# Moving weight splits and convolution taps in the vector queue of a decoder step that TensorE bounds

## What is computed

```python
def conv_ffn(xn, buf, w_up, conv_w, conv_b, w_down):
    u = xn @ w_up                       # 1024 -> 2 x 3072
    g, v = u[..., :D_FF], u[..., D_FF:]
    gc, new_buf = causal_dwconv(g, buf, conv_w, conv_b)   # width 3, along the tokens
    return (jax.nn.gelu(gc) * v) @ w_down, new_buf.astype(buf.dtype)
```

## Time and profile before

| | us |
|---|---|
| median of 3 runs | 2318.5 |
| lowest and highest | 2316.89, 2319.08 |
| the profiled execution: own time | 2320.66 |
| its span, first to last instruction | 2318.6 |
| busy PE, weight loads of PE | 2293.2, 2235.5 |
| busy DVE, ACT, POOL | 1646.1, 1013.8, 1107.9 |

### The profile page before, as it was taken

One profiled execution on the slowest core, in us unless ns is written; L12 is line 12 of the kernel. 1 busy time (PEld: TensorE's weight loads), 2 busy tenths in 40 slices (PEclk: granted clock), 3 DMA queues, 4 the chain that ended last, 5 costly groups with the idle time before them and its releaser, 6 DMA issues.

```text
span 2318.6 us, 43248 instructions
## 1 busy us (share of the span) xinstructions
PE 2293.2 (99%) x16916; PEld 2235.5 (96%) x16916; DVE 1646.1 (71%) x2172; ACT 1013.8 (44%) x1732; POOL 1107.9 (48%) x922
## 2 busy tenths in 40 slices
PE   8999999999999999999999999999999999999999
PEld 8999999999999999999999867999999999999999
DVE  7666547777777779986466675467777777789962
ACT  6555645333333334433354585453333333444331
POOL 3222466555555555656220153565555555566540
PEclk9999999999999999999999999999999999999999
DMA  4111122222222334322373202222221222254132
GB/s 136 46 46 46 51 100 83 73 67 83 83 74 65 112 101 172 118 84 77 121 105 86 65 18 96 99 70 84 83 82 57 84 83 84 81 194 142 56 103 91
DMA packets 228790, 203.04 MB, mean 88 GB/s; under 512 B 28373, under 2 KB 209821, under 8 KB 228412
## 3 DMA queue, kind: packets, MB, share of 16 engines
q1 hardware_dynamic: 224180, 188.87, 26.3%
q10 hardware_dynamic: 4404, 12.28, 2.2%
q0 software_dynamic: 64, 0.05, 0.0%
HBM read 152.41 MB, written 50.66 MB: 88 GB/s over the span
## 4 chain that ended last, share of the span: by engine, by line
PE 90%; DVE 4%; issue 2%; ACT 2%; POOL 1%; DMA 1%; SPq 0%; DVEq 0%; ACTq 0%; POOLq 0%
PE ps L1473 14%; PE ps L1472 14%; PE ps L1474 14%; PE ps L1230 9%; PE ps L1232 9%; PE ps L1231 9%; PE ps L1492 4%; PE ps L1493 4%; PE ps L1494 4%; PE ps L1713 1%; PE ps L1741 1%; PE ps L1765 1%; PE ps L1636 0%; DVE y L2977 0%; PE ps L1813 0%
## 5 line engine op out<-in xcount | busy, mean ns | idle before, releaser
L1492 PE MATMUL ps<-ring,later_slots 128*128 128x272 f32 x960 | 277.9, 289 | 4.3 <-DVE later_slots L2999 2.5
L1493 PE MATMUL ps<-ring,later_slots 128*128 128x272 f32 x960 | 276.6, 288 | 0.0
L1494 PE MATMUL ps<-ring,later_slots 128*128 128x272 f32 x960 | 274.8, 286 | 0.0
L2977 DVE SCALAR_TENSOR_TENSOR y<-convin,fcol,y 128x1024 f32<-128x1024 f32 x192 | 227.5, 1225 | 16.4 <-ACT y L2193 14.7
L1472 PE MATMUL ps<-b,slot_a 128*128 128x272 f32 x768 | 221.5, 288 | 1.8 <-DVE slot_a L2931 1.8
L1473 PE MATMUL ps<-b,slot_a 128*128 128x272 f32 x768 | 221.2, 288 | 0.0
L1474 PE MATMUL ps<-b,slot_a 128*128 128x272 f32 x768 | 220.5, 287 | 0.0
L1492 PEld LDWEIGHTS ps<-ring,later_slots 128*128 128x128 f32 x960 | 180.8, 188 | 6.3 <-DVE later_slots L2999 4.0
L1494 PEld LDWEIGHTS ps<-ring,later_slots 128*128 128x128 f32 x960 | 181.5, 189 | 0.0
L1493 PEld LDWEIGHTS ps<-ring,later_slots 128*128 128x128 f32 x960 | 181.5, 189 | 0.0
L1230 PE MATMUL ps<-sa,whi 128*128 128x384 f32 (+1 forms) x540 | 177.3, 328 | 1.4 <-DVE x L3036 1.3
(11 more groups left out here) (503 smaller groups left out, 7885.6 us busy)
## 6 DMA issues: line engine op xcount, KB each, us to landing
rawu<-in_f_w_up SPq DMA_DIRECT2D x192, 256.0 KB, 4.3
h_spill<-x SPq DMA_DIRECT2D x48, 544.0 KB, 3.1
down_raw<-in_f_w_down SPq DMA_DIRECT2D x48, 384.0 KB, 4.6
part<-h_spill SPq DMA_DIRECT2D x30, 544.0 KB, 5.0
f_spill<-x ACTq DMA_DIRECT2D x16, 544.0 KB, 2.7
x<-f_spill SPq DMA_DIRECT2D x16, 544.0 KB, 6.8
raw<-in_a_w_in SPq DMA_DIRECT2D x16, 512.0 KB, 4.1
last_rows<-h_spill SPq DMA_DIRECT2D x12, 544.0 KB, 4.9
```

Of the source, the lines that this page charges most:

```text
L1492: pe.matmul(out, slot[:, 0, i, :], b_hi, start=(i == 0 and not more), stop=False, skip_group_check=more)
L1493: pe.matmul(out, slot[:, 0, i, :], b_lo, start=False, stop=False, skip_group_check=more)
L1494: last = pe.matmul(out, slot[:, 1, i, :], b_hi, start=False, stop=(i == 2), skip_group_check=more)
L2977: ins = dve.scalar_tensor_tensor(out, g, fcol[:, u, col + t:col + t + 1], out, ALU.mult, ALU.add)
```

## The change

It alters the order of instructions on DVE and, in one place, on ACT. No instruction is added or removed, and PE's, POOL's and SP's programs are the same. In both layers:

1. Unit 0 (`entry`): the splits of slot_b (for T2) and slot_c (for T3) each go one token operand earlier.
2. Unit 1: the splits of slot_d and of slot_a (for B22) go between the two taps of unit 0's convolution, from behind them.
3. Last unit and first down steps: the fourth split of `first_slots`, the token operand B21 and the first split of `later_slots` go ahead of the whole last convolution. On ACT the fourth `first_slots` copy goes ahead of the B21 copy, and the last GeLU one step later. The T1 operand goes one step earlier, `make_hidden` one later.
4. Ahead of the plain block: both weight splits (`prep`) go one down step earlier.

```diff
@@ ACT
                         newest_tap(layer, u)
+                        down_weight_hi(layer, 0, 0, 3)
                         down_combo_hi(layer, 0, "B21")
...
-                    if q < SB * NQ - 3:
+                    if 0 < q < SB * NQ - 3:
                         down_weight_hi(layer, (q + 3) // NQ, (q + 3) % NQ // 4, (q + 3) % 4)
-                    if q == 1:
+                    if q == 2:
                         gelu(layer, FT - 1)
@@ DVE, entry
                 combo_lo(layer, "T2", "three")
+                weight_lo(layer, 0, 4)
                 combo_lo(layer, "T2", 3)
-                weight_lo(layer, 0, 4)
...
+                weight_lo(layer, 0, 5)
                 combo_lo(layer, "T3", 3)
-                weight_lo(layer, 0, 5)
...
-                unit_conv(layer, 0)
+                unit_conv(layer, 0, (1,))
+                weight_lo(layer, 1, 6)
+                weight_lo(layer, 1, 3)
+                unit_conv(layer, 0, (0,))
@@ DVE, ffn
-                    weight_lo(layer, u, 6)
-                    weight_lo(layer, u, 3)
+                    if u > 1:
+                        weight_lo(layer, u, 6)
+                        weight_lo(layer, u, 3)
...
                         down_weight_lo(layer, 0, 0, 2)
-                        unit_conv(layer, u, (1,))
                         down_weight_lo(layer, 0, 0, 3)
                         down_combo_lo(layer, 0, "B21")
-                        unit_conv(layer, u, (0,))
+                        down_weight_lo(layer, 0, 1, 0)
+                        unit_conv(layer, u)
...
-                    if 0 < q < SB * NQ - 3:
+                    if 1 < q < SB * NQ - 3:
                         down_weight_lo(layer, (q + 3) // NQ, (q + 3) % NQ // 4, (q + 3) % 4)
                     if q == 3:
                         scale_gelu(layer, FT - 1)
-                    elif q == 4:
+                    elif q == 5:
                         make_hidden(layer, FT - 1)
-                    early_ones = {5: (0, "T1"), 7: (0, "B22"), 12: (0, "T2"), 15: (0, "T3"), 19: (0, "T4"),
+                    early_ones = {4: (0, "T1"), 7: (0, "B22"), 12: (0, "T2"), 15: (0, "T3"), 19: (0, "T4"),
...
-                        elif t > FB:
-                            if t == FB + 1:
+                        elif t < FB + 2:
+                            if t == FB:
                                 dve.wait_ge(w_lo, steps_done(layer, SB - 1, NP - 1, 3))
-                            prep(n0, t - FB - 1, FB * P)
+                            prep(n0, t - FB, FB * P)
```

## The result

The changed kernel takes 2325.74 us (median of 20 runs, 2322.08 to 2335.13), the kernel before 2319.11 (20 runs, 2316.48 to 2323.22). The ratio is 1.0027, with a 95% interval of 1.0019 to 1.0035. By the ratio that is 6.3 us slower (4.4 to 8.1), where 4.1 was forecast; the two medians lie 6.6 apart. The profiled execution of the change took 2325.32 us with a span of 2323.3.

The account below looks back on a forecast made before the run. PE, busy 2293.2 of 2318.6 us, bounds the kernel, leaving only 25 us of standstill; 2 x (0 + 0.8 + 0.55 + 0.7) = +4.1 us gave 2322.6 us as median, own range 2320.5 to 2325, overall range 2315.5 to 2326.

Parts of the forecast that it names:

- Step 1: Unit 0: T2 and T3 start earlier, but T4 still waits for slot_d's split; 0 per layer.
- Step 2: Unit 1: slot_a's wait goes, but later taps delay GeLU and `scale_gelu`, so PE waits for slot_b's split; +0.8 us per layer.
- lower bound of -0.7: Unit 1: the best case per layer, a gain of 0.7 us if slot_b is in time after all.
- Step 3: First down steps: early waits shrink, but DVE finishes the set later, delaying PE's step at 902.36; +0.55 us per layer.
- Step 4: Plain block: both `prep` splits now precede the third take, which releases PE; +0.7 us per layer.
- It costs the upper bounds: Unit 1, down steps, plain block: each loses one more POOL turn; +7.9 us, 2326.4 us, chance 0.12.
- It is faster: Unit 1 and down steps: waits go and aren't given back; -7.7 us, 2310.8 us, chance 0.10.

Follow-up runs that it names:

- The order with everything ahead: Kernel before with unit 1's slot_d and slot_a splits between the taps, product 1's copy and slot_b's copy and split ahead of GeLU/`scale_gelu`: 2318.14 against 2319.58.
- the late split: Kernel before with only the first `prep` split a down step earlier, the second left behind the third take: 2316.81 against 2319.13, ratio 0.999.
- step 1 alone: Kernel before with only unit 0's slot_b and slot_c splits one token operand earlier: one run, 2318.26 against a median of 2319.13.
- without step 2: Changed kernel with unit 1's slot_d and slot_a splits back behind both taps, against the kernel before: 2323.05 against 2319.29, ratio 1.0014.

## Why the prediction was right or wrong

The direction and the range held, the size was low: 6.3 us against 4.1, and the chances had "no change" ahead of "slower". That the median still lies in the range, 0.3 us under its upper end, is luck: the wait that cost most and the clock behind it were both missing from the sum. By its own steps:

- **Step 1 (0 per layer): right.** T4 starts where it did relative to the start of the program, and the wait at T2 that went was given back at T4 in both layers.
- **Step 2 (+0.8 per layer): wrong, and the largest miss.** The step that failed is "The loss of 0.73 at 393.79 goes ... slot_a is ready about 391.7, PE arrives at 393.1". The list of what B22 waits for had only slot_a in it. The copy by ACT, which ended 0.08 us before slot_a's split, stood behind the very GeLU that the next sentences move back by 1.2 us. The forecast followed the GeLU to DVE and not to ACT's own queue. The wait went up to 1.96 and 2.53 and cost 1.5 and 1.0, and the clock 1.5 and 1.3 more: 3.0 and 2.3 in place of 0.8. With the copy ahead of the GeLU the rest of the step's sum came out at 0.95 and 0.6, so its reasoning on DVE, POOL and slot_b was sound. The change shows it too: DVE's gap ahead of `scale_gelu` is 0.63 (0.7 forecast), and `scale_gelu` lasts 1.81 beside POOL's weight sum, which started ahead of it, as forecast. The order with everything ahead (-0.3 and -0.5) stayed inside the lower bound of -0.7.
- **Step 3 (+0.55 per layer): right at its place, +0.49 and about +0.4.** Alone it measured 1.0001 (-1.9 to +2.3 us), which fits the 0.9 of both layers and fits nothing as well. The turns of DVE and POOL were right to a few tenths: 1.47, 3.02, 2.98 and 1.72 for a forecast of 1.1, 3.1 (the operand, from 874.2 to 877.3), 2.7 and 1.73.
- **Step 4 (+0.7 per layer): right in the wait, +0.6 in both layers by the starts.** What it may have missed is again the clock: alone the step measured +3.0 us, of which the waits are 1.2, and its trace has one stretch at the lower clock that cost 1.6. In the profiled execution of the change neither wait of step 4 was followed by one.
- **The sum.** The parts alone give 3.7 + 0.2 + 3.0 = 6.9 for the 6.3 measured; they add, within what can be told. By the waits alone the change would cost about 4.5 (1.5 and 1.0 in unit 1, 0.5 and 0.4 at the down steps, 0.6 twice at the plain block).
- **The rivals.** "It costs the upper bounds" had a fitting time (2326.4) for reasons that didn't happen: none of the three places lost one more POOL turn. "It is faster" named slot_b's split in unit 1 as the place that decides; it came at 398.16, two microseconds after the 396.1 that the rival asked for, and PE (T2 at 400.34) didn't wait for it only because it was held elsewhere for longer.

That DVE and POOL take exclusive turns is what the Trainium skill states on the page "SBUF — State Buffer", section "Who interferes with whom". The traces of the change agree at each new pair: the B21 operand lasts 3.02 and ends 1.7 after the last of POOL's three additions (879.11), and a `prep` split lasts 1.47 behind POOL's addition and 0.94 where it came ahead of it.

## What to carry to other kernels

Before moving an item past another, list everything that the bound engine waits for at that place, not only the one that the trace names, and look for those that end within a tenth of a microsecond of it; then follow the moved item in the queues of every engine that waits for it. On a queue without a gap, a reorder picks the customer that waits, and a gain comes from putting what the bound engine needs first ahead of what it needs later (all of unit 1's ahead), or from a better turn between two engines that take turns (the late split, 1.77 to 0.94). And price a longer wait of TensorE with what may follow it in clock, which in unit 1 was as much again as the wait.

## What was unexpected of the hardware

The clock of TensorE fell behind waits that are short. Leaving out the first 20 us of the program, the granted clock in the 4 us behind PE's waits was 1.00 for all 88 waits of 0.8 to 1.65 us in the 13 profiled executions here; of eight waits of 1.86, one was followed by the level of 1.2 GHz, of six from 1.96 to 2.25 four, and of the four from 2.53 to 2.60 all. Each such stretch lasted some 3 us and cost 1.3 to 1.6, unless PE had to wait soon after it anyway. The same wait in the same place, 1.86 ahead of the plain block of layer 1, had it in one kernel and not in three others, so with one profiled execution each it looks like chance.

A long wait is not the only thing in front of such a stretch. In four of the 13 executions one came at about 364 us, in layer 0, where PE had had no wait for over 70 us. Here it is with step 1 alone (PE alone, columns as above), where the kernel before has 1.00 and 30 matmuls:

```profile
364.50:368.00 3.50, 3.50 (x18) 0.51 0.02 5
```

In the first 20 us it doesn't go by the length of the wait either: a wait of 2.08 had 1.00 behind it (the late split alone) and one of 0.97 had 0.50 (without step 2). What decides stays open.
